# An encoder layer's MLP in fast matrix multiplication: the order of VectorE's and ScalarE's work, the refill of the weight slots, and the sample's part of one product

## What is computed

```python
h2 = rms_norm(x, ln2_w)
x = x + jnp.square(jax.nn.relu(h2 @ w_up)) @ w_down      # w_up (1024, 4096), w_down (4096, 1024)
```

## Time and profile before

| what | value |
|---|---|
| median of 3 runs | 1522.82 us (1519.46 to 1523.36) |
| the profiled execution: its own time | 1517.21 us |
| its span, first to last instruction | 1515.4 us |
| mean granted TensorE clock, share of full | 0.979 |
| busy: PE, PE weight loads | 1433.9 us (95%), 1265.7 us (84%) |
| busy: DVE, ACT, POOL | 947.2 us (63%), 593.2 us (39%), 131.6 us (9%) |
| loads of weight quarters | 64 of 1 MB on SP's queue |
| chain that ended last | PE 77%, DVE 12%, issue 6%, ACT 4% |

### The profile page before, as it was taken

The page is one execution under the profiler, slowest core; times in us unless marked ns, Lnnn a source line. Parts: engine busy times, 40 slices in busy tenths (PEclk is TensorE's granted clock), DMA queues, the critical chain, the costliest instruction groups (busy, mean ns, idle before and its releaser), DMA issues.

```text
span 1515.4 us, 22275 instructions
## 1 busy us (share of the span) xinstructions
PE 1433.9 (95%) x8198; PEld 1265.7 (84%) x8198; DVE 947.2 (63%) x1152; ACT 593.2 (39%) x743; POOL 131.6 (9%) x153
## 2 busy tenths in 40 slices
PE   8999999989899899899899999999899999999996
PEld 6888999889689788698688889988887887987985
DVE  6247335396866866867762562535877677677676
ACT  5212222264345345345442113214543543543553
POOL 2433000000000000000043330000000000000001
PEclk9999999999999999999999999999999999999998
DMA  7323111303203303304042221203113213203201
GB/s 254 126 84 113 63 56 57 112 15 112 96 17 112 111 1 112 111 16 153 2 148 97 88 81 63 93 25 121 72 41 111 73 40 111 84 28 112 87 26 70
DMA packets 74677, 124.72 MB, mean 82 GB/s; under 512 B 3332, under 2 KB 20868, under 8 KB 74568
## 3 DMA queue, kind: packets, MB, share of 16 engines
q1 hardware_dynamic: 74424, 123.18, 24.0%
q10 hardware_dynamic: 144, 0.07, 0.0%
HBM read 115.83 MB, written 7.41 MB: 81 GB/s over the span
## 4 chain that ended last, share of the span: by engine, by line
PE 77%; DVE 12%; issue 6%; ACT 4%; POOL 0%; DVEq 0%; DMA 0%; ACTq 0%; POOLq 0%
PE bank L612 22%; PE bank L770 15%; PE bank L622 11%; PE bank L863 11%; PE bank L784 7%; PE bank L876 5%; DVE raws L1798 4%; DVE ring L1775 3%; ACT ring L1132 3%; DVE x L1821 2%; PE bank L662 2%; DVE a_ring L1840 2%; PE bank L700 1%; PE bank L707 1%; PE bank L681 1%
## 5 line engine op out<-in xcount | busy, mean ns | idle before, releaser
L1132 ACT ACTIVATE ring<-raws 128x1024 fp32r<-128x1024 f32 x220 | 231.1, 1055 | 372.6 <-DVE raws L1798 124.3
L1775 DVE TENSOR_TENSOR ring<-raws,ring 128x1024 fp32r<-128x1024 f32 x220 | 268.8, 1222 | 169.2 <-ACT ring L1132 168.3
L863 PE MATMUL bank<-ring,a_ring 128*128 128x512 f32 x1344 | 318.1, 394 | 17.5 <-DVE a_ring L1840 17.5
L770 PE MATMUL bank<-mlp_in_hi,ring 128*128 128x256 f32 x1728 | 320.0, 283 | 0.0
L863 PEld LDWEIGHTS bank<-ring,a_ring 128*128 128x128 f32 x1344 | 254.1, 190 | 74.1 <-issue 20.8
L770 PEld LDWEIGHTS bank<-mlp_in_hi,ring 128*128 128x128 f32 x1728 | 272.1, 191 | 1.4
L770 PE MATMUL bank<-mlp_in_lo,ring 128*128 128x256 f32 x864 | 244.0, 282 | 0.0
L770 PEld LDWEIGHTS bank<-mlp_in_lo,ring 128*128 128x128 f32 x864 | 165.0, 191 | 1.4
L1798 DVE TENSOR_TENSOR raws<-raws 128x1024 f32<-128x1024 f32 x128 | 155.7, 1217 | 0.0
L1359 POOL TENSOR_SCALAR var<-sums 128x1 f32<-128x1 f32 x25 | 9.7, 386 | 1216.4 <-ACT xn L946 1212.8
L622 PE MATMUL bank<-norm_hi,ring 128*128 128x320 f32 x512 | 114.5, 310 | 0.0
(11 more groups left out here) (179 smaller groups left out, 2092.9 us busy)
## 6 DMA issues: line engine op xcount, KB each, us to landing
raws<-in_w_mlp_up SPq DMA_DIRECT2D x32, 1024.0 KB, 7.3
raws<-in_w_mlp_down SPq DMA_DIRECT2D x32, 1024.0 KB, 7.1
w_raw<-in_w_in SPq DMA_DIRECT2D x28, 1024.0 KB, 5.4
w_raw<-in_w_out SPq DMA_DIRECT2D x8, 1024.0 KB, 5.0
past_state<-in_state_ret SPq DMA_DIRECT2D x8, 512.0 KB, 5.1
out_ret_s<-past_state SPq DMA_DIRECT2D x8, 512.0 KB, 4.9
x<-in_x_prompt SPq DMA_DIRECT2D x4, 512.0 KB, 12.5
norm_row<-in_norm_rows SPq DMA_DIRECT2D x3, 512.0 KB, 3.6
```

Source lines behind the costliest of these rows:

```text
L770: mm = pe.matmul(cols, item_half(item, h, a)[:, k, n * P:(n + 1) * P], mlp_in[i][c][:, k], start=(i in (B11, B21, SUM_1112) and (n, k, m) ...
L863: mm = pe.matmul(out[:], a_item[:, a, 2 * h + k, pair * P:(pair + 1) * P], item_half(item, h, c)[:, k], start=(i in (B11, B21, SUM_1112) a ...
L1132: nc.scalar.activation(item_half(item, h, 0), raw_half(quad, RAW_OF[i], h), ACT.Copy).then_inc(half_hi.sem, 1)
L1775: nc.vector.tensor_tensor(item_half(item, h, 1), raw_half(quad, RAW_OF[i], h), f(item_half(item, h, 0)), ALU.subtract).then_inc(half_lo.se ...
```

## The change

1. ACT's and DVE's instructions of `up` and `down` stand in another order. The work itself is the same. In a block, DVE's two `weight_sum`s of `SUM_1112` for the next quad stand at the end of the phase before, except in the first block of a layer.
2. SP loads quarter "12" before "21" and each quarter into the slot that the matching item has left. `SLOTS` repeats after three quads instead of four.
3. PE computes the sample's part of product `B22` (number 5) in `up` ahead of the two halves for the prompt, not after them. Each half of that item is then free as soon as its prompt half is through.
4. `tail` and `sample_hidden` share their bytes.

```diff
@@ -114,18 +114,17 @@
 ITEMS = QUADS * PRODUCTS
-SLOTS = [(0, 1, 2, 3), (2, 3, 1, 0), (1, 0, 3, 2), (3, 2, 0, 1)]
+SLOTS = [(0, 1, 3, 2), (3, 1, 2, 0), (2, 1, 0, 3)]
...
 def slot_of(quad, name):
-    return SLOTS[quad % 4][("11", "12", "21", "22").index(name)]
+    return SLOTS[quad % 3][("11", "12", "21", "22").index(name)]
...
@@ -136,13 +135,13 @@
 for i in range(PRODUCTS):
-    if i == SUM_1222:
+    if i in (SUM_1222, B22):
         out.append(("up sample", b, i))
...
     out.append(("up", b, i, 1))
-    if i in (B11, B21, B22):
+    if i in (B11, B21):
         out.append(("up sample", b, i))
...
@@ -164,14 +163,13 @@
     if quad % 2 == 0:
-        return STEP["up sample", b, i] if i in (B11, B21, B22) else STEP["up", b, i, h]
+        return STEP["up sample", b, i] if i in (B11, B21) else STEP["up", b, i, h]
     return STEP["down sample", b, i] if i in (B11, B21) else STEP["down", b, i, h, 1]
...
-X_ADDS = ([(B11, p) for p in range(2)] + [(B21, p) for p in range(2)] + [(B21, "sample")]
-          + [(i, p) for i in (SUM_1112, SUM_111222) for p in range(2)]
-          + [(SUM_1222, p) for p in range(2)] + [(B22, "sample")]
+X_ADDS = ([(B11, p) for p in range(2)] + [(B21, "sample")]
+          + [(i, p) for i in (B21, SUM_1112, SUM_111222, SUM_1222) for p in range(2)] + [(B22, "sample")]
           + [(i, p) for i in (B22, SUM_ALL) for p in range(2)])
...
@@ -270,7 +268,9 @@
 ret_state = place("ret_state", [P, H, HD], f32, ret_at + 2 * KB)
-sample_hidden = place("sample_hidden", [P, 2, 512], f32)
+spare_at = region(4 * KB)
+sample_hidden = place("sample_hidden", [P, 2, 512], f32, spare_at)
+tail = place("tail", [P, FT, 2 + 2 * NB], f32, spare_at)
...
@@ -537,7 +536,7 @@
 settle(sp)
-for name in ("11", "21", "12", "22"):
+for name in ("11", "12", "21", "22"):
     load_quarter(layer, 0, name)
...
@@ -546,15 +545,11 @@
     load_quarter(layer, quad, "11")
-    sp.wait_ge(half_lo.sem, half_lo.at(layer, 2 * (first + SUM_1222) + 2))
-    settle(sp)
-    load_quarter(layer, quad, "21")
-    sp.wait_ge(half_lo.sem, half_lo.at(layer, 2 * (first + B22) + 2))
-    settle(sp)
-    load_quarter(layer, quad, "12")
-    sp.wait_ge(half_lo.sem, half_lo.at(layer, 2 * (first + SUM_ALL) + 2))
-    settle(sp)
-    load_quarter(layer, quad, "22")
+    for i, name in ((SUM_1222, "12"), (B22, "21"), (SUM_ALL, "22")):
+        sp.wait_ge(half_lo.sem, half_lo.at(layer, 2 * (first + i) + 2))
+        settle(sp)
+        load_quarter(layer, quad, name)
 sp.wait_ge(step_done.sem, step_done.at(layer, STEP["up", NBLK - 1, SUM_ALL, 1] + 1))
...
@@ -799,6 +794,9 @@
     pe.wait_ge(sample_relu.sem, sample_relu.at(layer, 2 * b + 1))
+if i == B22 and b == 0:
+    pe.wait_ge(in_diff_lo.sem, in_diff_lo.at(layer, 4))
+if i in (SUM_1222, B22):
     up_sample(b, i)
...
@@ -1251,29 +1249,29 @@
 copy_product(b, B11, 0)
-weight_half(item + 2, 0)
 copy_product(b, B11, 1)
 if b == 0:
...
     in_diff_hi_of(0)
+weight_half(item + 2, 0)
 weight_half(item + 2, 1)
-weight_half(item + 3, 0)
 if b == 0:
...
     in_diff_hi_of(2)
+square_hidden(b, h11, B21, 1.0)
+weight_half(item + 3, 0)
+weight_half(item + 3, 1)
 sample_square(b, 0)
-weight_half(item + 3, 1)
-square_hidden(b, h11, B21, 1.0)
 weight_half(item + 4, 0)
 if b == 0:
...
     in_diff_hi_of(4)
+weight_half(item + 4, 1)
 read_back(b, 0)
-weight_half(item + 4, 1)
-copy_product(b, SUM_111222, 0)
 a_item_hi(b, B11)
 weight_half(item + 5, 0)
+copy_product(b, SUM_111222, 0)
 copy_product(b, SUM_111222, 1)
 weight_half(item + 5, 1)
 copy_product(b, SUM_1222, 0)
@@ -1281,34 +1279,34 @@
     copy_product(b, SUM_1222, 1)
     weight_half(item + 6, 1)
     square_hidden(b, h22, SUM_1222, -1.0)
+    sample_square(b, 1)
     weight_half(item + 7, 0)
-    sample_square(b, 1)
+    weight_half(item + 7, 1)
     square_hidden(b, h12, B22, -1.0)
-    weight_half(item + 7, 1)
-    read_back(b, 1)
     a_item_hi(b, B21)
     weight_half(item + 8, 0)
+    read_back(b, 1)
 def down(b):
...
     weight_half(item + 1, 1)
     mid_diff_hi(b)
+    a_item_hi(b, SUM_1112)
     weight_half(item + 2, 0)
-    a_item_hi(b, SUM_1112)
     weight_half(item + 2, 1)
+    a_item_hi(b, SUM_111222)
     weight_half(item + 3, 0)
-    a_item_hi(b, SUM_111222)
     weight_half(item + 3, 1)
     weight_half(item + 4, 0)
+    weight_half(item + 4, 1)
     a_item_hi(b, SUM_1222)
-    weight_half(item + 4, 1)
     weight_half(item + 5, 0)
+    weight_half(item + 5, 1)
     a_item_hi(b, B22)
-    weight_half(item + 5, 1)
     weight_half(item + 6, 0)
+    weight_half(item + 6, 1)
     a_item_hi(b, SUM_ALL)
-    weight_half(item + 6, 1)
     if b < NBLK - 1:
         weight_half(item + 7, 0)
         weight_half(item + 7, 1)
@@ -1777,25 +1775,17 @@
 def weight_sum(quad, i, h):
-    a, b = {SUM_1112: ("11", "12"), SUM_111222: ("11", "22"), SUM_1222: ("12", "22"),
-            SUM_ALL: ("11", "21")}[i]
-    if i == SUM_1112:
-        slot = slot_of(quad, "12")
-        dve.wait_ge(slot_in[slot].sem, slot_in[slot].at(layer, 16 * (quad + 1)))
-    elif i == SUM_111222:
-        slot = slot_of(quad, "22")
-        dve.wait_ge(slot_in[slot].sem, slot_in[slot].at(layer, 16 * (quad + 1)))
-    before = {SUM_1112: B11, SUM_111222: SUM_1112, SUM_ALL: SUM_111222}
-    if i in before:
-        dve.wait_ge(half_lo.sem, half_lo.at(layer, 2 * (quad * PRODUCTS + before[i]) + h + 1))
-    if i == SUM_ALL:
-        dve.wait_ge(half_lo.sem, half_lo.at(layer, 2 * (quad * PRODUCTS + B21) + h + 1))
+    onto, name = {SUM_1112: ("11", "12"), SUM_111222: ("11", "22"), SUM_1222: ("12", "22"),
+                  SUM_ALL: ("11", "21")}[i]
+    slot = slot_of(quad, name)
+    dve.wait_ge(slot_in[slot].sem, slot_in[slot].at(layer, 16 * (quad + 1)))
+    if i == SUM_1222:
+        dve.wait_ge(weights_summed.sem, weights_summed.at(layer, sums_to(quad, SUM_1112, h)))
     else:
-        n = SUMS.index((i, h)) + quad * len(SUMS)
-        if i in (SUM_111222, SUM_1222):
-            dve.wait_ge(weights_summed.sem, weights_summed.at(layer, sums_to(quad, SUM_1112, h)))
-    out = raw_half(quad, a, h)
-    nc.vector.tensor_tensor(out, out, raw_half(quad, b, h), ALU.add).then_inc(weights_summed.sem, 1)
+        before = {SUM_1112: B11, SUM_111222: SUM_1112, SUM_ALL: SUM_111222}[i]
+        dve.wait_ge(half_lo.sem, half_lo.at(layer, 2 * (quad * PRODUCTS + before) + h + 1))
+    out = raw_half(quad, onto, h)
+    nc.vector.tensor_tensor(out, out, raw_half(quad, name, h), ALU.add).then_inc(weights_summed.sem, 1)
 def hidden_sum(b, i, h):
...
@@ -1895,104 +1885,104 @@
         weight_half(1, 0)
-    weight_sum(q, SUM_1112, 0)
+        weight_sum(q, SUM_1112, 0)
     weight_half(item + 1, 1)
     if b == 0:
+        weight_sum(q, SUM_1112, 1)
         read_turn_lo(layer, ("n2", NT - 2, 1))
-    weight_sum(q, SUM_1112, 1)
-    weight_half(item + 2, 0)
-    if b == 0:
         read_turn_lo(layer, ("n2", NT - 1, 1))
         in_diff_lo_of(0)
+        in_difference(0)
+        in_difference(1)
+    weight_half(item + 2, 0)
     weight_half(item + 2, 1)
...
     if b == 0:
-        in_difference(0)
-        in_difference(1)
-    hidden_sum(b, B21, 0)
-    weight_half(item + 3, 0)
-    hidden_sum(b, B21, 1)
-    weight_sum(q, SUM_111222, 1)
-    if b == 0:
         in_diff_lo_of(1)
         in_difference(2)
-    weight_half(item + 3, 1)
-    weight_sum(q, SUM_1222, 0)
+    hidden_sum(b, B21, 0)
+    weight_sum(q, SUM_111222, 1)
+    hidden_sum(b, B21, 1)
     if b == 0:
         in_diff_lo_of(2)
+    for h in range(2):
+        weight_sum(q, SUM_1222, h)
+    weight_half(item + 3, 0)
+    weight_half(item + 3, 1)
     weight_half(item + 4, 0)
-    weight_sum(q, SUM_1222, 1)
     if b == 0:
...
         in_diff_lo_of(4)
+    weight_half(item + 4, 1)
+    for h in range(2):
+        weight_sum(q, SUM_ALL, h)
     sample_lo(b, 0)
-    weight_half(item + 4, 1)
-    weight_sum(q, SUM_ALL, 0)
+    a_item_lo(b, B11)
     weight_half(item + 5, 0)
-    a_item_lo(b, B11)
-    weight_sum(q, SUM_ALL, 1)
     weight_half(item + 5, 1)
...
     weight_half(item + 6, 0)
...
     weight_half(item + 6, 1)
     hidden_sum(b, B22, 0)
+    weight_half(item + 7, 0)
+    weight_sum(q + 1, SUM_1112, 0)
     hidden_sum(b, B22, 1)
-    weight_half(item + 7, 0)
     weight_half(item + 7, 1)
-    sample_lo(b, 1)
+    weight_sum(q + 1, SUM_1112, 1)
     a_item_lo(b, B21)
     weight_half(item + 8, 0)
+    sample_lo(b, 1)
 def down(b):
     q, item = 2 * b + 1, (2 * b + 1) * PRODUCTS
-    weight_sum(q, SUM_1112, 0)
+    a_difference(b, SUM_1112)
     weight_half(item + 1, 1)
-    a_difference(b, SUM_1112)
-    sample_lo(b, 2)
-    weight_half(item + 2, 0)
     a_difference(b, SUM_1222)
     for p in range(2):
         add_to_x(b, B11, p)
-    weight_sum(q, SUM_1112, 1)
     a_item_lo(b, SUM_1112)
+    a_difference(b, SUM_111222)
+    weight_half(item + 2, 0)
+    weight_half(item + 2, 1)
     weight_sum(q, SUM_111222, 0)
-    weight_half(item + 2, 1)
-    a_difference(b, SUM_111222)
+    weight_sum(q, SUM_111222, 1)
```

(40 more changed lines are left out.)

## The result

| | before | after |
|---|---|---|
| median | 1521.14 us, 4 runs (1517.62 to 1523.36) | 1443.61 us, 4 runs (1443.22 to 1444.57) |
| ratio after / before | | **0.9493**, 95% interval 0.9472 to 0.9515 |
| profiled execution, its span | 1517.21 us, 1515.4 us | 1443.22 us, 1441.4 us |
| mean granted clock | 0.979 | 0.991 |

The change makes the kernel 77.5 us faster. In the profiled executions it is 74.0 us; the working of the prediction said 74.2.

A forecast was written before the change was run, and what follows sets the result against it. PE was taken to wait in gaps released by DVE, which has time in total but runs bunched work in order. Block savings of 74.2 us took 1517.2 to 1443.0 us profiled; half the median's excess made 1446, range 1437 to 1455.

The forecast's parts named there:

- The block without gaps: A block that is not a layer's first: without PE's three gaps and the slower matmuls behind them it takes 101.4 us.
- Down: Down phase: the gaps of 2.19 and 3.56 us go; tightest room 0.5 us, at the add of SUM_111222.
- SP's load of "12": Refill after down's SUM_ALL sums: "12" lands at T+94.4, its sum is due at T+95.3, T+100.6 would still do; cost nothing.
- In up: Up phase: the 1.77 us gap goes; smallest room 2.1 us, at the sample's transposes after ACT's sample_square.
- The first block: A layer's first block: the 4.00 us gap becomes one of 5.5 us one product earlier; the block takes 111.3 us.
- The clock: PE's slower matmuls after the 1.78 us gap come back too; by the skill page's rule they would not, giving 1451 us.
- The sum, term by term: Whole kernel: layer 0 gives 5.3 and 28.8 us, layer 1 6.2 and 33.9, together 74.2 us.
- I add half: From profiled time to median: half of the 5.6 us by which the median before exceeded its profiled time, giving 1446 us.
- (a): Rival, down: DVE stays the bound; one gap kept in each down gives 1464 or 1487 us; chance 0.14.
- (b): Rival, up: squares ahead of SUM_111222 hurt every block, not only the first; 1493 us; chance 0.04.
- (c): Rival, refill: the load of "12" holds DVE and stops PE; slower, over 1523 us; chance 0.03.
- (d): Rival, a layer's first block: it is better than forecast; 16 us less, 1430 us; chance 0.06.

The follow-up runs named there:

- e5: The changed kernel with DVE's low part of SUM_111222 in down made twice (one instruction more): 1453.0 us.
- e3: The changed kernel with the old SLOTS and the old order of loads (11, 21, 12, 22): 1445.1 us.
- e7: The changed kernel with ACT's high part of the first half of SUM_111222 in up made four times (three instructions more): 1458.9 us.
- e8: The changed kernel with an order of its own for ACT and DVE in the up phase of a layer's first block: 1426.9 us.
- e1: The kernel before with only the sample's part of B22 moved ahead of its two halves in up: 1522.6 us.
- e4: The changed kernel with DVE's two sums of SUM_1112 for down back at the start of down: 1454.5 us.
- e9: The changed kernel with DVE's low part of SUM_111222 in down made three times (two instructions more): 1463.1 us.
- e2: The changed kernel with the sample's part of B22 in up behind its halves again: 1474.4 us.
- e6: The changed kernel with DVE's low part of SUM_111222 in down made four times (three instructions more): 1474.6 us.
- e10: The changed kernel with DVE's low part of SUM_111222 in down made five times (four instructions more): 1486.9 us.

## Why the prediction was right

**The block without gaps.** I put it at 101.4 us; it is 101.15. The 0.3 between them is the slower product behind a gap: in the kernel before, the product after the 2.19 us gap took 5.73 us, not 5.44, and I had not taken that off.

**Down.** The order was written out against a PE that never waits. The timeline of DVE in the third block of layer 0, which starts at 517.0, so T+61 is 578:

```profile
580.62 4.63 DVE L1788 TENSOR_TENSOR raws<-raws 128x1024 f32<-128x1024 f32 x4
...
588.03 2.36 DVE L1773 TENSOR_TENSOR ring<-raws,ring 128x1024 fp32r<-128x1024 f32 x2
...
595.50 1.29 DVE L1811 TENSOR_TENSOR x<-x,bank 128x512 f32<-128x512 f32 x2
...
597.83 1.28 DVE L1811 TENSOR_TENSOR x<-x,bank 128x512 f32<-128x512 f32 x2
...
611.09 1.23 DVE L1773 TENSOR_TENSOR ring<-raws,ring 128x1024 fp32r<-128x1024 f32 x1 [2.07 <-ACT ring L1130]
612.94 1.22 DVE L1788 TENSOR_TENSOR raws<-raws 128x1024 f32<-128x1024 f32 x1 [0.62 <-DMA raws<-in_w_mlp_up]
```

```profile
577.20:588.00 10.80, 10.80 (x50) 8.94 (x49) 10.60 (x10) 5.09 (x5) 0.00 (x0) 1.00 0.01 2
588.00:604.00 16.00, 16.00 (x72) 13.25 (x71) 15.93 (x19) 7.21 (x7) 0.00 (x0) 1.00 0.00 0
```

The first low half of SUM_111222 starts at 588.03 and with 1.22 us is through at T+72.25 (counted: 72.3). The first add of SUM_111222 starts at 597.83 and is followed by the next 0.60 later, T+81.4 (counted 81.6, due 82.1; PE starts the product at 598.97, T+81.97). From 577.2 to 604.0 DVE is busy for 26.5 of 26.8 us, as densely as before the change, and in its timeline nothing longer than a pause of 0.20 us stands between T+61 and T+92. What changed is what stands at the front of that run. e5 shows the room from the other side.

**The rest of the terms.** SP's load of "12" came later than counted: DVE waited 0.62 us for it at 612.94, T+95.9, where I had it landed at 94.4. It cost nothing, as said, since T+100.6 would do; e3 puts a wait of up to 4.1 us there at next to no price. In up there are 2.0 us of room (counted 2.1, e7). The first block lost its gap of 4.00 us and got one of 5.73 one product earlier (counted 5.5). The timeline of ACT in it shows the chain of the count:

```profile
330.28 1.06 ACT L1157 ACTIVATE hidden<-hidden 128x1024 f32<-128x1024 f32 x1 [6.12 <-DVE hidden L1797]
...
332.33 1.99 ACT L1130 ACTIVATE ring<-raws 128x1024 fp32r<-128x1024 f32 x2
334.22 0.58 ACT L1178 ACTIVATE sample_hidden<-bank 128x512 f32<-128x512 f32 x1
334.83 0.63 ACT L1180 ACTIVATE sample_hidden<-sample_hidden 128x512 f32<-128x512 f32 x1
```

The square of h11 starts 0.4 us later than counted, and all behind it follows: two squares, two high halves, and sample_square, whose end at 335.46 (counted 335.2) releases PE. PE's work behind the gap then takes 1.8 us longer than without it in layer 0 and 2.1 in layer 1 (counted 2.1). The block takes 111.1 us (counted 111.3). That the gap is only an effect of the order is shown by e8, which removes it.

**The clock.** The Trainium skill's section HAM oscillation, on the page TensorE: Matmul & The Clock Gate, lays the fall on longer idle gaps than the 1.78 us of up, and by it layer 1's later blocks would have stayed slower than counted. The rows speak against that: they took 112.7 us and now take 101.15, the same as in layer 0, at a granted clock of 1.00. The change took all three gaps of a block away at once; that the loss stands right behind the 1.78 us gap is seen in the earlier trace rows and in e1, where the clock is 0.63 there.

**The sum, term by term.** That 74.0 us fit the 74.2 counted to 0.2 is in part luck. The first blocks gave 5.5 and 6.2 us (counted 5.3 and 6.2), the later blocks of layer 0 28.8 (28.8), the rest of layer 1 34.7 (33.9). Between them, from the end of layer 0's MLP to the start of layer 1's, the changed kernel is 1.2 us slower, where I counted nothing. There PE idles for 2.0 us ahead of the next layer (1.9 before), and the twelve matmuls behind that took 4.58 us in this execution at a granted clock of 0.62, 3.02 before at 1.00: the same loss behind an equal gap as in e1, now on the other side.

**What was off.** One step: "I add half", the 2.8 us between the profiled execution and the median. The runs of the changed kernel lie within 1.4 us where those of before spread over 5.7, and the median is 0.4 above the profiled time. More of the scatter went with the gaps than half; without that step the forecast is 1443.0 for a median of 1443.6. The direction of the argument was right, as e1's trace shows, and its size was off. And the view that the price of a gap is its length and a loss of clock was incomplete, as e5 showed: 0.3 us in the product behind it and 0.1 us until PE starts belong to it, at a full clock.

**The rivals.** (a) does not hold for this order, but is near: e4 and e5 turn it on with 2.3 and 1.2 us more. (b) and (c) are excluded by the changed kernel's own trace: PE has no gap at the transposes of a later block, and DVE waits for a load for 1.0 us at most, ACT for 2.3, without PE being late. e7 and e3 show how much more of either it would take. (d) was not the case: the first block is as counted, and e8 makes it faster only by a further change.

## What to carry to other kernels

When an engine has spare time in total and the bottleneck still waits for it, write out for one period when each of its steps can run and when its result is due, and order by the due times; DVE's same 80 us of work in a block then fit without a gap. Give the first period its own order if it has other work, since an order that is right for the steady state can make the start worse. A part that brings nothing alone (e1) can be worth 31 us behind another one (e2), so judge it by taking it out of the whole.

## What the runs showed of the hardware that was not expected

A gap of PE costs more than its length, and how much more is not set by the length alone. Behind gaps of 0.9 to 1.0 us (e4, e5, e9) and behind the 2.19 us gap of the kernel before, the next product took 5.71 to 5.76 us instead of 5.44; in the blocks read for it, one or two of each of these kernels, the granted clock was 1.00. Behind the 2.25 to 2.28 us gaps of e2 and e6 it took 7.2 to 7.4 us in 13 of 16 blocks and 5.7 to 5.8 in the other three. Behind equal gaps of 3.53 us in e10 it took 5.73 us in one block, 7.1 to 7.4 in five, and 8.26 and 8.49 in two. The same 1.78 us gap in up cost 0.26 us in layer 0 and 1.85 in layer 1 in the kernel before, and 1.85 in both layers in e1, where the same matmuls stand around it. Where the time is lost, the granted clock of the window is 0.62 to 0.67, a mean of the two levels of 1.2 and 2.4 GHz. What decides whether the clock falls behind an equal gap was not tested.

Part of the scatter of the runs is this. e1's profiled execution is 4.5 us longer than that of the kernel before, for losses behind equal gaps. The kernel before ran in 1512.4 to 1523.8 us over all the comparisons, the changed one in 1443.2 to 1444.6. That the smaller spread comes from the missing gaps fits this, but was not tested by itself.
